# Sixteen products of constants removed from TensorE's program in a two-block transformer kernel

## The reference

```python
for i in range(2):                       # first block, layers 0 and 1
    sh1, sc1, g1, sh2, sc2, g2 = ada_modulation(c, w_ada[i], b_ada[i])
    h = rmsnorm(x, norm_mix[i]) * (1 + sc1) + sh1
    o = gla_mixer(h, hc, ...) if i == 0 else mla_mixer(h, hc, ...)
    x = x + g1 * o
    x = x + g2 * conv_ffn(modulate(x, norm_ffn[i], sh2, sc2), ...)
...
h = rms_norm(x, mix_norm_g)              # second block
mixed = concat(attn, c, mo)              # dilated attention, a convolution, memory attention
h = h + mixed @ w_out
h = h + ffn(rms_norm(h, ffn_norm_g))     # 1024 -> 2 x 2816 -> 1024
```

## Time and profile before

| what | value |
|---|---|
| median of 3 runs | 1290.04 us |
| profiled execution, its own time | 1289.77 us |
| its span, first to last instruction | 1287.5 us |
| granted clock, mean over the span | 0.997 |
| TensorE busy | 1253.9 us (97%), 7648 products |
| GpSimd, ScalarE, VectorE busy | 714.8, 709.3, 585.2 us |

### The profile page before, as it was taken

How to read it: one execution, slowest core, us unless ns; L and a number is a source line. 1 busy time by engine, 2 the same in 40 slices (tenths; PEclk the granted TensorE clock), 3 DMA queues, 4 the chain that set the end, 5 groups by cost and what they waited for, 6 DMA issues and landing times.

```text
span 1287.5 us, 21221 instructions
## 1 busy us (share of the span) xinstructions
PE 1253.9 (97%) x7648; PEld 1068.7 (83%) x7648; DVE 585.2 (45%) x1081; ACT 709.3 (55%) x1091; POOL 714.8 (56%) x335
## 2 busy tenths in 40 slices
PE   5999999999999999999999999999999999999999
PEld 1688678787888888888767658899999977999998
DVE  3425672237444444201065464555543585666621
ACT  3572356336554445422267454777775767877752
POOL 0442234353544444544435034688899874988897
PEclk8999999999999999999999999999999999999999
DMA  9523753742333323633623334555666540665564
GB/s 359 198 96 111 277 199 131 279 164 80 99 103 109 98 98 99 244 105 111 227 106 117 129 132 164 191 196 195 195 214 202 180 142 33 220 196 196 199 204 129
DMA packets 60130, 210.11 MB, mean 163 GB/s; under 512 B 6433, under 2 KB 9761, under 8 KB 59937
## 3 DMA queue, kind: packets, MB, share of 16 engines
q1 hardware_dynamic: 59632, 207.52, 47.2%
q10 hardware_dynamic: 432, 1.70, 0.3%
HBM read 208.15 MB, written 1.05 MB: 162 GB/s over the span
## 4 chain that ended last, share of the span: by engine, by line
PE 73%; POOL 12%; issue 6%; DVE 4%; ACT 3%; DMA 2%; SPq 0%; POOLq 0%; DVEq 0%; ACTq 0%
PE ps L387 52%; POOL wlo L374 11%; PE ps L407 3%; PE ps L525 2%; DMA raw<-wstream 2%; PE ps L408 1%; PE ps L1644 1%; PE ps L1623 1%; PE ps L1222 1%; PE ps L453 1%; PE ps L1210 1%; ACT whi L369 1%; PE ps L435 1%; PE ps L445 1%; PE ps L1190 1%
## 5 line engine op out<-in xcount | busy, mean ns | idle before, releaser
L374 POOL TENSOR_TENSOR wlo<-raw,whi 128x1024 fp32r<-128x1024 f32 x291 | 686.8, 2381 | 498.3 <-ACT whi L369 498.2
L369 ACT ACTIVATE whi<-raw 128x1024 fp32r<-128x1024 f32 x291 | 306.7, 1057 | 190.1 <-PE ps L387 94.5
L387 PE MATMUL ps<-Hhi_,whi 128*128 128x256 f32 (+1 forms) x1328 | 376.9, 314 | 0.1
L387 PE MATMUL ps<-Hlo_,whi 128*128 128x256 f32 (+1 forms) x1328 | 373.5, 311 | 0.0
L387 PEld LDWEIGHTS ps<-Hhi_,whi 128*128 128x128 f32 x1328 | 253.7, 191 | 16.2 <-issue 4.1
L387 PEld LDWEIGHTS ps<-Hlo_,whi 128*128 128x128 f32 x1328 | 254.2, 191 | 13.3 <-issue 1.4
L387 PE MATMUL ps<-Hhi_,wlo 128*128 128x256 f32 (+1 forms) x1328 | 223.1, 311 | 0.3 <-POOL wlo L374 0.3
L387 PEld LDWEIGHTS ps<-Hhi_,wlo 128*128 128x128 f32 x1328 | 192.5, 191 | 12.5 <-POOL wlo L374 0.4
L829 ACT ACTIVATE u<-ps,par 128x256 f32<-128x256 f32 (+1 forms) x132 | 82.6, 626 | 82.5 <-PE ps L387 78.2
L407 PE MATMUL ps<-hid,whi 128*128 128x512 f32 x352 | 115.8, 383 | 0.2 <-DVE hid L897 0.2
L880 DVE SCALAR_TENSOR_TENSOR u<-ps,par,u 128x255 f32<-128x255 f32 (+1 forms) x132 | 73.2, 555 | 81.1 <-ACT u L829 81.0
(11 more groups left out here) (346 smaller groups left out, 1774.4 us busy)
## 6 DMA issues: line engine op xcount, KB each, us to landing
raw<-wstream SPq DMA_DIRECT2D x367, 512.0 KB, 3.5
Haside_lo<-wstream SPq DMA_DIRECT2D x8, 512.0 KB, 6.0
Haside_hi<-wstream SPq DMA_DIRECT2D x8, 512.0 KB, 9.0
Paside<-wstream SPq DMA_DIRECT2D x4, 512.0 KB, 4.9
XT<-x_t SPq DMA_DIRECT2D x1, 1024.0 KB, 10.8
XT<-ctx_t SPq DMA_DIRECT2D x1, 1024.0 KB, 12.8
memx<-mem_t ACTq DMA_DIRECT2D x1, 1024.0 KB, 5.3
out_t<-XT SPq DMA_DIRECT2D x1, 640.0 KB, 6.4
```

Of the source, the lines that this page charges most:

```text
L369: nc.scalar.activation(whi[:, n % RING, :], raw[:, r % RAWS, :], ACT.Copy).then_inc(S["hi_ready"], 1)
L374: nc.gpsimd.tensor_tensor(wlo[:, r, :], raw[:, r, :], whi[:, n % RING, :].bitcast(F32), ALU.subtract).then_inc(S["lo_ready"], 1)
L387: mm = nc.tensor.matmul(o, a, b, start=start, stop=stop)
```

## The change

All six places of `keep_running` go, with the function itself and its two tables. Sixteen calls of matmul leave TensorE's program. No wait, no other instruction, and nothing of another engine is touched.

```diff
-IDLE_BEFORE = {"smix": (1, 4)}
...
-IDLE_AFTER = {"ffn0": (0, 2), "mix1": (7, 2), "ffn1": (0, 2)}
...
-        def keep_running(pe, bank, count):
-
-            for _ in range(count):
-                nc.tensor.matmul(ps[:, bank, 0:T], ones, con[:, 0:T], start=True, stop=True)
...
             mod_products(pe, 0, 2)
-            keep_running(pe, 0, 2)
             mod_turn(pe, 0)
-            keep_running(pe, 0, 4)
...
                             pe.wait_ge(S["e_lo"], KD)
-                        if st in IDLE_BEFORE:
-                            keep_running(pe, *IDLE_BEFORE[st])
                         norm_pe(pe, st, norms(st)[st][2])
                         if st in UNIT_AFTER:
                             mod_products(pe, 1, *UNIT_AFTER[st])
-                        if st in IDLE_AFTER:
-                            keep_running(pe, *IDLE_AFTER[st])
```

## The result

| what | before | changed |
|---|---|---|
| median, 22 runs each | 1289.82 us | 1291.54 us |
| range of the runs | 1289.15 to 1292.12 | 1290.26 to 1293.67 |
| profiled execution, its span | 1289.77, 1287.5 | 1293.67, 1291.4 |
| mean granted clock of the profiled execution | 0.997 | 0.995 |

The ratio is 1.0013, with a 95% interval from 1.0007 to 1.0019: slower by about 1.7 us. The range forecast held it (1288.9 to 1292.8), the forecast itself, 0.12 us faster, did not: this is rival A. The changed kernel's profiled execution is the slowest of its 22, so its 3.9 us over the kernel before are more than the usual loss. The lines of the changed kernel are numbered a little lower: L451 is the old L453, L518 the old L525, L537 the old L544, L545 the old L552, L715 the old L724.

What follows compares the result with a forecast made beforehand. It took TensorE, holding 73% of the span, as the bound. Savings of 0.10 at the turn and 0.02 at smix, zero elsewhere, made 0.12 us less than the median 1290.04: 1289.9 us, range 1288.9 to 1292.8.

Steps and rivals of the forecast that it cites:

- rival A: Head, pause 31.0 to 33.7 us: the clock falls, costing 1.3 to 3.4 us, 2.0 taken, giving 1291.9; chance 0.22.
- I take the clock to stay: All places: the granted clock stays at 1.00 despite the emptier pauses, so no clock loss; chance 0.68.
- the prediction's own sign of being wrong: Whole kernel: clock falls once more and median above 1292, or the stretch 28 to 34 shorter by over half a microsecond.
- The turn: Head, two calls ahead of mod_turn: its first product starts sooner, saving 0.10 us, between 0 and 0.20.
- ffn0, mix1, ffn1: Calls at these three places: hidden by waits, so removal saves 0; mix1 between 0 and 0.10 us.
- smix: Four calls ahead of norm_pe: they overhang the wait, so removal saves 0.02 us, between 0 and 0.20.
- Rival C: All places: the removed products were on the path, so 8.4 us come back, giving 1281.5; chance 0.02.
- B: Head, ffn0, mix1, ffn1, smix: clock falls at all five, costing 10 us at 2.0 each, giving 1299.9; chance 0.04.
- the price of missing cover: Each place: without the wait hiding them, products would cost their own time, 1.97 us behind the turn, 1.13 at ffn0.

Runs made afterwards that it cites:

- e10: Kernel before, without the calls ahead of the turn and at smix, two of four behind the turn replaced by two real modulation slots: ratio 1.0002.
- e3: Kernel before, with only the four calls behind the head's turn removed: 1291.38 us, ratio 1.0014.
- e1: Kernel before, with all six calls in the head removed and the other four places kept: 1291.94 us, ratio 1.0016.
- e4: Kernel before, with only the two calls ahead of the head's turn removed: 1289.59 us, ratio 1.0003.
- e2: Kernel before, with the ten calls at ffn0, mix1, ffn1 and smix removed and the head kept: 1289.95 us, ratio 1.0001.
- e8: Kernel before, with only two of the sixteen calls kept, behind the head's turn: 1291.70 us, ratio 1.0012.
- e5: Kernel before, with four more calls at each of ffn0, mix1, ffn1 and smix: 1292.99 us, one run, no ratio.
- e9: Kernel before, with only four of the sixteen calls kept, behind the head's turn: 1289.81 us, ratio 0.9999.
- e6: Changed kernel, with two real slots of modulation unit 3 moved up behind the head's turn: 1291.00 us, ratio 1.0009 to the kernel before.
- e7: Kernel before, with two of the four calls behind the head's turn replaced by two real slots of modulation unit 3: 1289.51 us, ratio 0.9994.

## Why the prediction was wrong

**The one step that failed is "I take the clock to stay".** The prediction named the mechanism, its place and its sign as rival A and gave it 0.22; it gave 0.68 to a held clock. The runs showed a second fall, at 34.1 us in the profiled execution, and 6.8 us at 0.50 behind it, 2.80 us between the two biases.

The step rested on two rows of one execution. The first is a stretch of 2.0 us with 0.75 busy that kept the clock, set against one of 4.5 us with 0.9 busy. That is no like for like: a pause is to be compared with one of its own length, and by length the head's was nearer to the one that had lost the clock. Nor is the place of that row safe: e10 lost the clock behind it when the wait there was 2.08 us instead of 1.25. The second is the pause that lost the clock, against which 2.7 us seemed short. The same pause lost it 2.0 us after the last product in e3, and in e1 only 5.4 us after it (12.82, and the fall at 18.2). A single fall gives no length that is safe, and a single row without one doesn't either: one execution shows that the clock held there, not that it always does.

**Rival A's price was about right.** 1.3 to 3.4 us, 2.0 taken, gave 1291.9; measured 1291.54. The range held the result only since it was drawn wide enough for A, and the prediction's own sign of being wrong asked for a fall and a median above 1292, of which only the fall came. The low stretch cost 2.80 us between the biases where it lasted 6.8 us (changed kernel), 2.42 where part of it fell into the pause (e1), 1.59 at half the length (e3). The runs of the changed kernel part the same way: six at 0.996 with a median of 1290.94, 1.1 over before, and fifteen at 0.995 with 1291.78, 2.0 over.

**The rest of the sum held.** The turn: 0.10 forecast, 0.09 to 0.10 found (e4). ffn0, mix1, ffn1: 0 forecast; e2 is at 1.0001, and none of the four places moved in the changed trace. smix: 0.02 gain forecast, 0.03 loss found: L696 starts 0.15 us behind its total instead of 0.20, but L698 starts 0.51 behind L696 instead of 0.43. Rival C (8.4 us faster) and B (all places) fell; but the four other places aren't safe for good, as e8 shows for ffn1.

**What was weak though it came out:** the price of missing cover. e5 shows that a pause's length bounds the cover from below only.

The Trainium skill's advice (TensorE: Matmul & The Clock Gate, "Why this matters for your kernels") is against long pauses between bursts of products, and the prediction read it as speaking against the change. In direction the runs agree: e1 and e3 lost the clock, e2 and e4 didn't show a loss. But the pause without any product, 2.64 us, was shorter than those the page warns of, so read to the letter it foretold neither this fall nor the one behind 1.30 us in e8; the measurement decides.

Open stay: why the low stretch is 6.8 us in one execution and 3.3 in another, where the clock fell in the runs that were not profiled, whether three calls would do, and what share of runs loses the clock at ffn1 or at 252 us.

## What to carry to other kernels

Before taking useless work off an engine that waits, ask of each place two things apart: does the next instruction wait for it (no: its time is worth nothing), and is it all that keeps the engine's clock. Judge the second by the longest near-empty stretch that would arise, a turn like the head's counted as empty for safety, against rows of the same length, and not by one execution: the same wait kept the clock in four traces and lost it in a fifth. Price it by what follows: 1 to 3 us here, since TensorE leads for the 6 us behind the pause. And put filling where the pause is longest: four of sixteen calls did all the work that these runs can tell.

## What the runs showed of the hardware

- With TensorE idle for 2.64 or 2.65 us ahead of its first real product, and only a turn of 8-column products before that, the granted clock dropped to 0.50 in all three profiled executions (changed, e1, e3), and none of these kernels' 44 runs has the mean of 0.997. With two calls of filling (idle 1.68 us, e8) the profiled execution kept it in the head, and six of eleven runs have 0.995 and a loss of 2.3 us. With four (0.82 us, e4 and e9) three of 22 runs are below 0.997, against three of 81 of the kernel before. It is a matter of chances between runs, not one limit.
- The fall doesn't stand at a fixed distance from the last product: in the first pause it came from 2.0 us (e3) to 5.4 us (e1) after it, and later on it came when real products had been back for 1.5 us (e3), 1.6 (e6), 1.8 (e8) and 1.2 (e10).
- What a low stretch costs goes by who leads behind it: 3.3 us at 0.50 cost 1.59 us in the head (e3) and 1.70 at 252 us (e10), where TensorE is busy throughout, and 0.4 at ffn1 (e8), where VectorE leads at full clock.
- A slot of a modulation unit is two calls, four records of 128x512. Alone it takes 1.05 us, and two slots back to back take 1.06 in all (e7, and 34.30 in the kernel before). Splitting the two doubled their time on TensorE.
- A chain of waits that names removable work (1.06 us of constants in the earlier trace rows) named the wrong predecessor: with the constants gone, the copy on ScalarE stood in their place at the same time, and 0.10 was left.
